# Three out-projections by seven half-width products, and memory squares added on VectorE

## What is computed

```python
# first block, layers i = 0 and 1 (mixer_ab and mixer_cd end alike)
return jnp.concatenate([oa, ob], axis=-1) @ w_out          # 1024 -> 1024
x = x + mixer(...)
x = x + memory_cross_attention(rms_norm(x, g_xq[i]), rms_norm(mem, g_mem[i]), ...)
x = x + swiglu(rms_norm(x, g_ffn[i]), w_gate_up[i], w_down[i])
# second block
x = x + merged @ w_out[l]                                  # 1024 -> 1024
x = x + cross_attention(rms_norm_2(x, norm_xattn[l]), mem_n, ...)
x = x + conv_ffn(...)
return rms_norm_2(x, norm_final)
def rms_norm(x, g):  # y = x * rsqrt(mean(x*x) + EPS) * g
```

## Time and profile before

| | |
|---|---|
| median of 3 runs | 3054.28 us (3052.68 to 3055.96) |
| the profiled execution, its own time | 3054.26 us |
| its span in the trace | 3052.1 us |
| mean granted TensorE clock | 0.994 of full speed |
| TensorE (PE) busy | 96% |
| VectorE (DVE) busy | 49% |
| ScalarE (ACT) busy | 20% |
| ring units loaded | 395 of 512 KB |

### The profile page before, as it was taken

The page is one execution under the profiler, slowest core; times in us unless marked ns, Lnnn a source line. Parts: engine busy times, 40 slices in busy tenths (PEclk is TensorE's granted clock), DMA queues, the critical chain, the costliest instruction groups (busy, mean ns, idle before and its releaser), DMA issues. The chain is left out here.

```text
span 3052.1 us, 34848 instructions
## 1 busy us (share of the span) xinstructions
PE 2945.1 (96%) x14152; PEld 1916.8 (63%) x14152; DVE 1502.9 (49%) x3053; ACT 614.0 (20%) x1289; POOL 0.3 (0%) x5
## 2 busy tenths in 40 slices
PE   8989999999999999999999999999999999999997
PEld 3545488888544454888885445466654544688886
DVE  4652454453326534566646973444441203566653
ACT  3450310100115503100000021422220102222200
POOL 0000000000000000000000000000000000000000
PEclk9999999999999999999999999999999999999999
DMA  4012122222220222222221111211112231222222
GB/s 141 28 41 84 62 83 83 96 91 97 76 69 31 66 90 76 83 83 83 83 97 62 56 56 56 69 43 36 43 43 85 94 97 55 76 83 89 91 83 76
DMA packets 61936, 224.30 MB, mean 73 GB/s; under 512 B 6992, under 2 KB 7120, under 8 KB 61264
## 3 DMA queue, kind: packets, MB, share of 16 engines
q1 hardware_dynamic: 61776, 222.07, 21.8%
HBM read 219.95 MB, written 2.10 MB: 73 GB/s over the span
## 5 line engine op out<-in xcount | busy, mean ns | idle before, releaser
L935 PE MATMUL ps<-h,ring 128*128 128x512 f32 x784 | 357.0, 602 | 2.5 <-PEq L2801 2.5
L935 PEld LDWEIGHTS ps<-h,ring 128*128 128x128 f32 x784 | 144.4, 191 | 169.3 <-issue 164.8
L1383 PE MATMUL ps<-h,ring 128*128 128x256 f32 x1008 | 240.5, 382 | 6.1 <-DVE u L1405 4.6
L1383 PE MATMUL ps<-h_sums,w_sums 128*128 128x256 f32 x1008 | 224.4, 379 | 0.0
L1383 PEld LDWEIGHTS ps<-h,ring 128*128 128x128 f32 x1008 | 192.2, 191 | 35.5 <-DVE u L1405 5.7
L923 PE MATMUL ps<-h,ring 128*128 128x512 f32 x480 | 208.4, 592 | 0.0
L1383 PEld LDWEIGHTS ps<-h_sums,w_sums 128*128 128x128 f32 x1008 | 191.8, 190 | 25.8
L923 PEld LDWEIGHTS ps<-h,ring 128*128 128x128 f32 x480 | 91.3, 190 | 112.6 <-issue 111.1
L981 DVE TENSOR_TENSOR x<-x,ps 128x512 f32<-128x512 f32 x48 | 33.0, 688 | 226.4 <-PE ps L923 226.4
L599 PE MATMUL ps<-hid_sums,d_sums 128*128 128x256 f32 x528 | 121.8, 379 | 0.0
L923 PE MATMUL ps<-o_x,ring 128*128 128x512 f32 x256 | 110.6, 593 | 3.7 <-PEq L1130 3.7
(11 more groups left out here) (547 smaller groups left out, 4563.2 us busy)
## 6 DMA issues: line engine op xcount, KB each, us to landing
ring<-stream_dram SPq DMA_DIRECT2D x395, 512.0 KB, 3.6
bias<-bias_dram SPq DMA_DIRECT2D x8, 448.0 KB, 4.9
mem<-mem_dram SPq DMA_DIRECT2D x3, 1024.0 KB, 5.1
x<-x_dram SPq DMA_DIRECT2D x4, 512.0 KB, 7.4
out_dram<-x SPq DMA_DIRECT2D x8, 256.0 KB, 2.2
rope_ab<-ropes_dram SPq DMA_DIRECT2D x4, 256.0 KB, 9.1
s_big<-s_big_dram SPq DMA_DIRECT2D x1, 1024.0 KB, 4.9
constants<-constants_dram SPq DMA_DIRECT2D x1, 768.0 KB, 12.1
```

The costliest lines, as they stand in the source:

```text
L935: mm = pe.matmul(out, w, r, start=(k == 0), stop=(k == len(rhs) - 1))
L1383: mm = pe.matmul(ps[:, bank + at, 0:256], w(k), x(k), start=start and k == 0, stop=k == 3, skip_group_check=not start)
```

## The change

The three out-projections run through `Down`, which now takes its operand as two halves of any number of k-tiles and the places of its buffers. With four k-tiles in a half there is one chunk to a pair: four chunks in all. The weights of the three matrices are packed as those of the down projections and start at a unit. The memory squares are added over their eight tiles by one VectorE `tensor_reduce` behind `combine(0)`, so that one matmul of 256 columns is left of eight; it stands behind pair 1, in the free half of bank 3, and the memory's root and scaling behind `combine(1)`. In every `Down`, `squares` of the pair before now stand ahead of `combine(q)`. The core of the diff:

```diff
-    w.put(every(a['w_out_ab'][0][np.concatenate([pairs, 512 + pairs])]))
+    w.align(UNIT_BLOCKS)
+    w.put(pack_down(a['w_out_ab'][0][np.concatenate([pairs, 512 + pairs])]))
...
+DOWN_KB = 44, 77, 93, 128
...
-    CHUNKS = [slice(0, 4), slice(4, 8), slice(8, 11)]
-    def __init__(self, net, hid, gain=None, second=None):
+    def __init__(self, net, top, bottom, kb, gain=None, second=None):
+        self.chunks = [slice(k, min(k + 4, half)) for k in range(0, half, 4)]
+    def done(self, q, n):
+        return (len(self.chunks) + 3) * q + len(self.chunks) - 1 + n
+
+    def order(self, q, c):
+
+        if c == 0 and (q == 0 or len(self.chunks) > 1):
+            return 1, 2, 3, 5, 6, 4, 7
+        return 1, 6, 5, 7, 2, 4, 3
...
-            for n, name in enumerate((1, 2, 3, 5, 6, 4, 7) if c == 0 else (1, 6, 7, 5, 2, 4, 3)):
+            order, last = self.order(q, c), c == n_chunks - 1
+            closes = {4: 1, 6: 3} if order[1] == 2 else {1: 1, 3: 1, 5: 1, 6: 1}
+            summed = False
+            for n, name in enumerate(order):
                 at, w, x = products[name]
-                if name == 3 or c and n == 1:
+                if name in (3, 5, 6, 7) and not summed:
                     pe.wait_ge(*s['w_sum'].at(g + 1))
+                    summed = True
...
+                if name == 3 and before_last:
+                    before_last(q)
...
+            if last and between:
+                between(q)
...
-        for g in range(3 * self.PAIRS):
-            if g + 1 < 3 * self.PAIRS:
+        for g in range(n_chunks * self.PAIRS):
+            if g + 1 < n_chunks * self.PAIRS:
                 weights(g + 1)
...
-            if g % 3 == 2:
-                q = g // 3
-                combine(q)
+            if g % n_chunks == n_chunks - 1:
+                q = g // n_chunks
...
                 for m in range(max(2 * q - 2, 1), 2 * q):
                     squares(m)
+                combine(q)
+                if between:
+                    between(q)
...
-                for m in range(DT):
-                    self.residual_pe(pe, m, src)
-                    if m == 3:
-                        for i in range(DT):
-                            pe.wait_ge(*s['m_sq'].at(i + 1))
-                            mm = pe.matmul(ps[:, 4, 0:MEM], self.c('ones'), msq[:, i, :], start=(i == 0), stop=(i == DT - 1))
-                        mm.then_inc(*s['m_sum'].up())
+                def memory_sum(q):
+                    if q == 1:
+                        pe.wait_ge(*s['d_freed'].at(1))
+                        pe.wait_ge(*s['m_acc'].at(1))
+                        pe.matmul(ps[:, 3, MEM:S], self.c('ones'), m_acc[:, :], start=True, stop=True,
+                                  skip_group_check=True).then_inc(*s['m_sum'].up())
+
+                def memory_read(q):
+                    if q == 2:
+                        pe.wait_ge(*s['m_read'].at(1))
+                out.pe(pe, memory_sum, memory_read)
                 for n in range(nh):
                     if n < 4:
-                        pe.wait_ge(*s['x_add'].at(n + 5))
+                        pe.wait_ge(*s['d_freed'].at(3))
...
                     if n == 0:
+                        pe.wait_ge(*s['d_freed'].at(4))
                         self.root_pe(pe, 5)
...
+                def memory(m):
+                    if m == 0:
                         act.wait_ge(*s['m_in'].at(16))
                         for i in range(DT):
                             act.activation(msq[:, i, :], mem[:, i, :], ACT.Square).then_inc(*s['m_sq'].up())
+                    if m == 4:
                         act.wait_ge(*s['m_sum'].at(1))
...
+                def memory(q):
+                    if q == 0:
+                        dve.wait_ge(*s['m_sq'].at(DT))
+                        dve.tensor_reduce(m_acc[:, :], msq[:, :, :].rearrange("p k m -> p m k"), AX.X, ALU.add).then_inc(*s['m_acc'].up())
+                    if q == 1:
                         dve.wait_ge(*s['m_ln'].at(1))
+                        dve.tensor_scalar(m_ms[:, :], ps[:, 3, MEM:S], 1.0 / D, EPS, ALU.mult, ALU.add).then_inc(*s['m_read'].up())
...
+                out.dve(dve, memory)
                 self.root_dve(dve, 5, ms[:, :], w[:, :])
```

More of the change, by code:

```diff
@@ L157, in put_first_block @@
     w.put(pack_rows(m[:, 1440:1952]))
[L158 removed]
+    w.align(UNIT_BLOCKS)
+    w.put(pack_down(a['w_out_cd'][0]))
     put_cross(w, a['w_xq'][1], a['w_xkv'][1], a['w_xo'][1])
@@ L545, in __init__ @@
         self.atok = net.place('pair_atok', [P, 4, P], 138)
+DOWN_KB = 44, 77, 93, 128
 class Down:
-    CHUNKS = [slice(0, 4), slice(4, 8), slice(8, 11)]
     PAIRS = DT // 2
-    def __init__(self, net, hid, gain=None, second=None):
-        p, tag = net.place, net.names
+    def __init__(self, net, top, bottom, kb, gain=None, second=None):
+        p, tag, half = net.place, net.names, top.shape[1]
         net.names += 1
[L559 to L562, removed]
+        self.net, self.s, self.top, self.bottom, self.gain, self.second = net, net.s, top, bottom, gain, second
+        self.chunks = [slice(k, min(k + 4, half)) for k in range(0, half, 4)]
+        self.ts, self.sums = p(f'hid_sums{tag}', [P, 3, half, 256], kb[0]), p(f'd_sums{tag}', [P, 2, 4, S], kb[1])
+        self.u, self.v = p(f'd_u2{tag}', [P, 256], kb[2]), p(f'd_u3{tag}', [P, 256], kb[2] + 1)
+        self.xsq = p(f'd_xsq{tag}', [P, 2, S], kb[3])
@@ L563, in __init__, with pe @@
         net.align(UNIT_BLOCKS)
         self.first = net.block_at // UNIT_BLOCKS
-    @staticmethod
-    def done(q, n):
-        return 6 * q + 2 + n
+    def done(self, q, n):
[4 more added lines that the diff above has]
+        return 1, 6, 5, 7, 2, 4, 3
     def region(self, q, j):
         return self.net.ps[:, 4 * (q % 2) + j // 2, 256 * (j % 2):256 * (j % 2) + 256]
-    def pe(self, pe):
-        net, s, hid, ts, sums, first = self.net, self.s, self.hid, self.ts, self.sums, self.first
+    def pe(self, pe, between=None, before_last=None):
+        net, s, ts, sums, first, n_chunks = self.net, self.s, self.ts, self.sums, self.first, len(self.chunks)
+        top_x, bottom_x = self.top, self.bottom
@@ L575, in pe @@
         lo, hi = slice(0, 256), slice(256, 512)
-        for g in range(3 * self.PAIRS):
-            q, c = divmod(g, 3)
+        for g in range(n_chunks * self.PAIRS):
+            q, c = divmod(g, n_chunks)
             top, bottom = net.pair_units(first, g)
-            sw, ks = sums[:, g % 2, :, :], range(self.CHUNKS[c].start, self.CHUNKS[c].stop)
+            sw, ks = sums[:, g % 2, :, :], range(self.chunks[c].start, self.chunks[c].stop)
             block_of = lambda w, k: w[:, k * P:(k + 1) * P]
@@ L602, in pe, with dve @@
                         net.unit_done(mm, first + 2 * g + 2)
-                    elif j == len(ks) - 1 and (n == 6 or c == 2 and n in (1, 3, 5)):
+                    elif j == len(ks) - 1 and last and n in closes:
+                        mm.then_inc(*s['w_p'].up(closes[n]))
+                    elif j == len(ks) - 1 and n == 6:
                         mm.then_inc(*s['w_p'].up())
[L605 to L609, removed]
+            if last and between:
+                between(q)
+        net.block_at = (first + 2 * n_chunks * self.PAIRS) * UNIT_BLOCKS
+        net.unit = first + 2 * n_chunks * self.PAIRS - 1
+    def dve(self, dve, between=None):
+        net, s, ts, sums, first, n_chunks = self.net, self.s, self.ts, self.sums, self.first, len(self.chunks)
         u, v, xsq, region, done = self.u, self.v, self.xsq, self.region, self.done
@@ L1032, in cross_inputs @@
         msq = p(f'mem_squares{tag}', [P, DT, MEM], 44)
-        m_rs, m_ms, m_w = (p(f'{n}{tag}', [P, MEM], 52 + j) for j, n in enumerate(('mem_root', 'mem_mean', 'mem_w')))
-        xsq = p(f'c_xsq{tag}', [P, 2, S], 100)
+        m_rs, m_ms, m_w, m_acc = (p(f'{n}{tag}', [P, MEM], 52 + j) for j, n in enumerate(('mem_root', 'mem_mean', 'mem_w', 'mem_sum')))
+        out = Down(self, *src)
         ms, w = p(f'c_mean{tag}', [P, S], 104), p(f'c_w{tag}', [P, S], 106)
@@ L1088, in _ @@
             def _(dve):
-                for m in range(DT):
-                    self.residual_dve(dve, m, xsq)
-                    if m == 4:
+                def memory(q):
[3 more added lines that the diff above has]
+                    if q == 1:
                         dve.wait_ge(*s['m_ln'].at(1))
-                        dve.tensor_scalar(m_ms[:, :], ps[:, 4, 0:MEM], 1.0 / D, EPS, ALU.mult, ALU.add).then_inc(*s['vec'].up())
+                        dve.tensor_scalar(m_ms[:, :], ps[:, 3, MEM:S], 1.0 / D, EPS, ALU.mult, ALU.add).then_inc(*s['m_read'].up())
                         dve.wait_ge(*s['m_root'].at(1))
-                        dve.wait_ge(*s['vec'].now())
+                        dve.wait_ge(*s['m_read'].at(1))
                         self.refine(dve, m_rs[:, :], m_ms[:, :], m_w[:, :])
@@ L2977, in _, with second_block @@
                 self.prefetch(sync)
```

(4 more changed lines are left out.)

54 lines of the change are left out of this document (27 added, 27 removed).

## The result

The changed kernel takes 3035.69 us (median of 4 runs, 3033.06 to 3036.16) against 3054.82 us of the kernel before in the same series: ratio 0.9935, 95% interval [0.992, 0.9951]. A second series gave 3037.75 against 3054.59, ratio 0.9941 [0.9926, 0.9956]. So the change gains 17 to 19 us where 29.6 were forecast; the time lies above the range. The profiled execution took 3033.06 us, with a span of 3030.9 at a mean clock of 0.993.

What follows compares the result with a forecast made beforehand. The prediction took TensorE to bound the out-projections. Three shorter TensorE lists, 28.8 us, plus 0.84 us for squares ahead of combine gave 29.6 us: 3054.3 - 29.6 = 3024.6 us, range 3022 to 3032.

Steps and rivals of the forecast that it cites:

- Transfers: Out-projections: eight units as before, two at a time, about 114 GB/s, four of the ring's five there at start; cost 0.
- up to 2.95 us: Out-projections: extra wait for each chunk's weight sums if the cover of the transfers went.
- TensorE's list: Each out-projection: 48.86 us instead of 58.46, saving 9.60 us, 28.8 us over all three.
- nothing is gained in the products: Rival, out-projections: half-width matmuls paced by weight loads or transfers; 3053 us, or 3044 with other gains; chance 0.04.
- The memory sums' 3.03: Each out-projection: us saved on TensorE by dropping seven of eight memory-sum matmuls.
- VectorE's list: Each out-projection: VectorE's work grows from 12.69 to some 45 us of 48.9, yet costs no time.
- the term: Reduce of memory squares in each out-projection: 2.28 us for 2048 elements, at the rate of earlier reduces.
- the 2.1 us of reserve: VectorE in each out-projection: time left of 48.9 us, which hides the reduce.
- the 14.2 us at which the kernel would have ended slower: Rival, out-projections: strided reduce so slow, 6.9 ns an element, that it cancels the 29.6 us gain; slow reduce's chance 0.03.
- VectorE becomes the bound: Rival, out-projections: VectorE's larger work exceeds its reserve; up to 3032 us, or 3042 with a 10 us reduce; chance 0.09.
- Squares ahead of combine: Last down projection: two squares run before combine, so the last root comes 0.84 us sooner; nothing counted for the other two.

Runs made afterwards that it cites:

- fillers: Unread matmuls ahead of the last down projection and last root: changed kernel with early ring release 3027.01 us, with tree of adds too 3025.92; kernel before 3054.36.
- the order alone: Kernel before with only the squares moved ahead of combine in the down projections: 3054.17 us, ratio 0.9997.
- the ring mended: Changed kernel, with the first matmul of each out-projection counting all earlier ring units as used: 3028.12 us, run again 3027.72 us.

## Why the prediction was wrong

The sign was right and the mechanism of the gain too; the size was wrong. The medians miss the forecast by 11.1 us (3035.69 against 3024.6). One step, the transfers, is 6.1 of them; the rest is in part the clock, and in part not attributed, as most runs left no trace.

- **Transfers: the step that failed.** The prediction put them at "Cost 0", as "four of the ring's five are there at the start". In the first and third stage that held. In the second, three of its own units were there; the fourth could not be issued before chunk 0 ended, 11.5 us in. That cost 6.1 us by the rows and went away with one signal. I had reckoned bytes (114 GB/s; the stages' windows show 108 to 120) and the order of the queue, but not what *permits* an issue. I also said that the alignment's zero blocks cost nothing, looking at their bytes; it is their unit boundary that took away the release. The bound I gave, "up to 2.95 us" a chunk, was the right size for the one wait (2.87), but I left it out of the range, and left out what VectorE's late start adds behind it (1.02 and 0.30, and 1.02 at the root).
- **TensorE's list: right.** Forecast 48.86 us from first product to keys; measured 48.86, and 48.85 in the third stage. Half-width products run at the pace of the down projection: the rival "nothing is gained in the products" is refuted. The memory sums' 3.03 was measured alone as 3.01 to 3.03.
- **VectorE's list: right in its reserve, wrong in the reduce.** The reduce took 3.70 us, 1.42 over the term; it took 1.4 of the 2.1 us of reserve, and nothing was lost in the two stages that had their units. The rate of the earlier trace rows was that of contiguous reads, and the strided 8 elements did not show the surcharge: at 0.70 ns an element it is 6 ns of 165. The error of the step was to take a row of 8 elements as evidence for 2048. The Trainium skill's rule (SBUF — State Buffer, "Door 1: The DMA port swizzle") says that access which leaves its 16-byte line pays at each crossing. The runs agree in direction: with 1024 bytes from read to read the reduce took 63% longer. No other stride was measured in it, so where the cost begins is not shown. It stayed far from the 14.2 us at which the kernel would have ended slower. The rival "VectorE becomes the bound" did not come about; doubling the reduce shows how near it was.
- **Squares ahead of combine: 0.8 us shown, and mostly not received.** The idle time fell as worked out, but without fillers the root's matmul ran at the low clock (2.02 to 2.08 us) in seven of the eight profiled executions with the change, and in the one of the order alone. In the eighth, with the memory sums on TensorE, it took 1.13 us, and the 0.8 us were received. In the one profiled execution of the kernel before it took 1.13 us after 3.50 us without work.
- **What the sum had no term for.** The start of the last down projection, partly at the low clock in every profiled execution without fillers: 5.32 us before and 5.89 with the order alone, 5.70 to 6.48 with the change (eight executions). The start of the third out-projection: at the low clock, and 1.7 us longer by it, in five of the ten profiled executions with the change and in none of the three of the kernel before and its variants. And some 0.15 us more of idle time at the start of each out-projection (1.20 us in the first two, 1.05 before).

With the ring mended, the time is 3027.8 us (the median of its 8 runs) against the 3024.6 forecast: within the range given.

What stays open: why the clock falls ahead of one root and not of another with as much or more idle time ahead of it, and how much of the low clock the changed kernel pays on average, as single runs vary by more than it.

## What to carry to other kernels

When a stage is repacked or aligned, write down for its first units what event lets each be issued, not only its bytes: a unit left half used by the stage before may have lost the instruction that released it. Where work is moved to an engine, subtract every moved instruction from its reserve at the next due time, and price a strided read only from a long strided read. A cut in the idle time ahead of a lone matmul may be paid back by the clock; compare that matmul's own duration before counting it.

## What the runs showed of the hardware

- A VectorE reduce of 2048 float32 from 1024 bytes apart took 3.70 us, of the same data side by side 2.28. ScalarE writing 256 elements 32 bytes apart took 681 ns, contiguous 401. Three halving adds took 1.22 + 0.69 + 0.42 us.
- TensorE's granted clock fell behind short pauses. After 6.6 us without work the next 16 records took 5.3 to 6.5 us (the slowest of these windows at 0.55 of full clock); after 1.9 us, 5.38 in five of the profiled executions with the change and 3.69 in the five others; after the fillers and 1.4 to 1.5 us, 3.69. The length of the pause does not decide by itself, as the last root shows: after 3.50 us in the kernel before the matmul took 1.13 us, at full clock; after 2.70 us it took 2.07 with the order of the squares alone, at the low level, and 1.13 with the memory sums on TensorE.
